# Two moves in the key scan: VectorE's product of slot 20 and GpSimd's page of slot 17

## The reference, cut to what matters

```python
z = x @ w_in                               # q | k | v | B | C | h
att  = block-sparse attention with ALiBi over q, k, v      # 8 heads x 64
conv = B * dwconv3_causal(C * h)                           # the mixer
x1 = layer_norm(alpha * x + concat(att, conv) @ w_out)
u  = dwconv3_causal(x1 @ w_ffn_up); a, g = split(u)
y  = layer_norm(alpha * x1 + (silu(a) * g) @ w_ffn_down)
```

```python
page_sum = jnp.sum(cache_k[layer, page_table], axis=2)     # all 16 pages of a sequence
gate = einsum('bthd,bnhd->bthn', q, kmean)                 # score of each block
_, sel = lax.top_k(gate, 3)
s = einsum(q, k_g) / 8 - slope * dist;  p = softmax(s);  out = einsum(p, v_g)
```

## Time and profile before

| | before |
|---|---|
| median of 3 runs | 438.33 us (438.18 to 438.52) |
| the profiled execution | 437.8 us |
| its span, first to last instruction | 436.0 us |
| mean granted TensorE clock | 0.993 |
| TensorE busy | 412.7 us (95%) |
| VectorE busy | 294.7 us (68%) |
| ScalarE busy | 181.4 us (42%) |
| GpSimd busy | 110.8 us (25%) |
| DMA | 124.60 MB, mean 286 GB/s |

### The profile page before, as it was taken

How to read it: one execution, slowest core, us unless ns; L and a number is a source line. 1 busy time by engine, 2 the same in 40 slices (tenths; PEclk the granted TensorE clock), 3 DMA queues, 4 the chain that set the end, 5 groups by cost and what they waited for, 6 DMA issues and landing times.

```text
span 436.0 us, 8237 instructions
## 1 busy us (share of the span) xinstructions
PE 412.7 (95%) x2903; PEld 339.2 (78%) x2903; DVE 294.7 (68%) x382; ACT 181.4 (42%) x694; POOL 110.8 (25%) x133
## 2 busy tenths in 40 slices
PE   4999999999999998999999989999999999999990
PEld 4588887876876774765653479999999999999990
DVE  0498999999799976954541275666776776534437
ACT  1587569644469133112110243554455555233201
POOL 1005334995255152200000717122211220000002
PEclk9999999999999999999999999999999999999997
DMA  8999999899999999999999953665556766676002
GB/s 313 397 359 407 405 407 393 316 404 409 409 359 327 338 404 405 406 405 404 402 405 398 318 196 98 194 191 162 158 169 191 213 181 186 183 211 206 3 2 99
DMA packets 109515, 124.60 MB, mean 286 GB/s; under 512 B 5903, under 2 KB 67048, under 8 KB 109466
## 3 DMA queue, kind: packets, MB, share of 16 engines
q1 hardware_dynamic: 101138, 107.30, 70.2%
q10 hardware_dynamic: 8336, 16.78, 10.2%
HBM read 121.65 MB, written 2.61 MB: 285 GB/s over the span
## 4 chain that ended last, share of the span: by engine, by line
PE 64%; DVE 18%; DMA 5%; issue 5%; SPq 4%; POOL 2%; ACT 1%; DVEq 0%; POOLq 0%; ACTq 0%
PE ps L1821 12%; PE ps L1822 11%; PE ps L1823 11%; PE ps L1714 8%; PE ps L1608 6%; DVE qk L939 6%; DVE T L949 5%; PE ps L1437 4%; PE ps L1632 4%; PE ps L1634 3%; PE ps L1384 3%; SPq L360 2%; DMA wring<-in_cache_v 2%; DMA KV<-in_cache_k 2%; POOL x1l L612 1%
## 5 line engine op out<-in xcount | busy, mean ns | idle before, releaser
L1188 DVE TENSOR_TENSOR wlo<-KV,whi 128x2048 fp32r<-128x2048 f32 (+1 forms) x24 | 61.7, 2571 | 57.5 <-ACT whi L838 29.3
L1437 PE MATMUL ps<-xT,wring 128*128 128x264 f32 x384 | 89.6, 388 | 0.1
L1437 PEld LDWEIGHTS ps<-xT,wring 128*128 128x128 f32 x384 | 71.6, 190 | 13.6 <-issue 1.7
L1821 PE MATMUL ps<-x1h,whi 128*128 128x264 f32 x256 | 73.7, 288 | 0.2
L1822 PE MATMUL ps<-x1l,whi 128*128 128x264 f32 x256 | 72.7, 284 | 0.0
L1823 PE MATMUL ps<-x1h,wlo 128*128 128x264 f32 x256 | 72.6, 284 | 0.0
L939 DVE TENSOR_TENSOR qk<-KV,qk 128x1536 f32<-128x1536 f32 (+1 forms) x32 | 67.0, 2097 | 6.6 <-DMA KV<-in_cache_k 2.7
L669 ACT ACTIVATE qk<-qk 128x64 f32<-128x64 f32 x216 | 51.9, 245 | 29.1 <-POOL qk L560 23.1
L949 DVE TENSOR_REDUCE T<-qk 128x24 f32<-128x1536 f32 (+1 forms) x32 | 58.4, 1827 | 0.0
L1821 PE MATMUL ps<-fh,whi 128*128 128x264 f32 x176 | 50.4, 286 | 0.1
L1822 PE MATMUL ps<-fl,whi 128*128 128x264 f32 x176 | 50.0, 284 | 0.0
(11 more groups left out here) (215 smaller groups left out, 574.0 us busy)
## 6 DMA issues: line engine op xcount, KB each, us to landing
KV<-in_cache_k SPq DMA_DIRECT2D x128, 256.0 KB, 6.2
KV<-in_w_ffn_up SPq DMA_DIRECT2D x32, 512.0 KB, 4.7
KV<-in_cache_v SPq DMA_DIRECT2D x60, 256.0 KB, 7.3
wring<-in_cache_v SPq DMA_DIRECT2D x56, 256.0 KB, 6.4
KV<-in_w_ffn_down SPq DMA_DIRECT2D x8, 1408.0 KB, 6.3
wring<-in_w_in ACTq DMA_DIRECT2D x5, 2048.0 KB, 14.0
zbuf<-in_cache_v SPq DMA_DIRECT2D x12, 256.0 KB, 5.3
zbuf<-in_w_ffn_up SPq DMA_DIRECT2D x3, 1024.0 KB, 10.2
```

The lines of the kernel that those rows point to most:

```text
L1188: nc.vector.tensor_tensor(wlo[s][:, 0:n], w2[s][:, 0:n], whi[s][:, 0:n], ALU.subtract).then_inc(s_lo, 1)
L1437: ins = nc.tensor.matmul(ps[:, z_bank(n), 0:R], tile[k], xT[:, k, :], start=k == 0, stop=k == KT - 1)
L1821: nc.tensor.matmul(out, wh[k], xh[k], start=k == 0, stop=False)
```

## The change

VectorE's program no longer makes the product of slot 20 as a part of `scan(19)`, after the weights of sequences 0 and 1. It makes it right after the sums of slot 18, ahead of the wait for the denominators; the sums of slot 19 stay where they were. GpSimd's program no longer multiplies its page of slot 17 after the mixer's last small products. It does so between the mixer's third tile (t = 2) and its fourth (t = 3). Nothing is added or removed.

```diff
@@ GpSimd
             for t in range(4):
+                if t == 3:
+                    multiply_page(17)
                 pool.wait_ge(s_ze, 12 + t + 1)
                 nc.gpsimd.tensor_tensor(zT[:, 20 + t, :], zT[:, 16 + t, :], zT[:, 20 + t, :], ALU.mult).then_inc(s_ch, 1)
...
                 chain(nc.gpsimd.tensor_tensor(cus, cus, cts, ALU.add))
-            multiply_page(17)
             multiply_page(18)
@@ VectorE
             probability_sums(0)
             reduce(18)
+            multiply(20)
             denominators(0)
             sample_weights(0)
             sample_weights(1)
-            scan(19)
+            reduce(19)
             own_weights(0)
             scan(20)
```

## The result

| | before | after |
|---|---|---|
| median of 18 runs each | 437.75 us (437.12 to 438.52) | 439.12 us (438.17 to 442.75) |
| ratio, 95% interval | | 1.0043 (1.0032 to 1.0055) |
| the profiled execution | 437.8 us | 438.66 us |
| its span | 436.0 us | 436.9 us |
| mean granted TensorE clock | 0.993 | 0.994 |

The change makes the kernel slower, by 1.4 us between the medians and 1.9 us by the ratio, which is of the means (0.0043 x 437.75; interval 1.4 to 2.4). The forecast was +0.81 us, and a median of 439.1.

The account below looks back on a forecast made before the run. The prediction took the wait chain through VectorE's penalties to TensorE as the bound, DMA queues second. Delays of +0.45 and +0.36 gave +0.81 us, from a median of 438.33 to 439.1; range 437.8 to 440.1.

Parts of the forecast that it names:

- Both collisions: VectorE and GpSimd meet at slot 17 and the penalties (+0.45 us), and at slot 22's product and L591 (+0.36).
- the sum of 0.81: TensorE's delays at the penalties, +0.45, and at the first value product, +0.36, add to +0.81 us.
- How a waiting engine gets in: Between VectorE and GpSimd, the first runs to its end; the other begins about 0.14 us before that recorded end.
- Edit 1, VectorE first: VectorE's slot 17 product runs first; the mixer's late steps hold the gate penalties: +0.45 us at TensorE; forecast's chance 0.40.
- nothing there is waited for: From 100 to 119 us TensorE has only 0.04 us of idle time, so work freed there brings no gain.
- Edit 1, GpSimd first: Rival: GpSimd's L566 goes first at 93.95, slot 17's product waits, penalties 0.9 to 1.2 us late; 439.7 us, chance 0.26.
- the tie: GpSimd's instruction behind slot 17's page (93.95) and VectorE's slot 17 product (93.94) fall due within 0.02 us; VectorE favoured.
- Edit 2: the mechanism: Slot 22's product, earlier at about 124.88, holds GpSimd's L591, for which TensorE's first value product waits: +0.36 us.
- The hole in the queues: DMA rate falls to 302 GB/s from 135 to 150 us; values 4 go out later, widening it by TensorE's delay.
- Both bounds move together: Delays to TensorE between 99.67 and 136 us also delay the refilling of the DMA queues.
- The rival that the queues gain: Key loads fill the DMA hole of 135 to 150 us: -1.1 us, 437.2, chance 0.11.

Follow-up runs that it names:

- Without its collision edit 2: Only edit 2 on the kernel before, with VectorE waiting for GpSimd's products with B ahead of the product of slot 22; 437.85 us, ratio 1.0007.
- edit 2: VectorE's product of slot 20 moved right behind slot 18's sums; alone against the kernel before: 438.6 us, ratio 1.0017.
- with the penalties out of the way as well: Both edits, gate penalties ahead of slot 16's sums, and VectorE waiting ahead of slot 22's product, against the kernel before; 437.99 us, ratio 1.0009.
- edit 1: GpSimd's page of slot 17 moved ahead of the mixer's fourth tile; alone against the kernel before: 438.3 us, ratio 1.0006.
- the page alone: The kernel before with only GpSimd's page of slot 17 moved, VectorE as before; 438.3 us, ratio 1.0006.
- the deliberate delay: The kernel before with one VectorE sum of the first gate's penalties made five times instead of once; 443.3 us, ratio 1.0134.
- the run with GpSimd first at slot 17: Both edits, with VectorE's product of slot 17 waiting for the first product of the mixer's last tile, against the kernel before; 440.0 us, ratio 1.0055.
- the run with VectorE first: Both edits, with GpSimd waiting for VectorE's product of slot 17 before the mixer's last tile, against the kernel before; 439.3 us, ratio 1.0037.

## Why the prediction was right, and where its sum was not

**Direction and place: right, shown.** Both collisions are where they were put, and the waits of TensorE with them. Without its collision edit 2 costs nothing that can be measured; with the penalties out of the way as well, both edits together cost nothing that can be told from noise (+0.4 us).

**The number: near in part by luck.** 439.1 was forecast and 439.12 measured, but the forecast started from 438.33, where the kernel before has 437.75 in these runs. The loss is 1.4 to 1.9, about twice the sum of 0.81. The 0.78 at the first value product is not the sum come true either: edit 1 brought 0.43, of which 0.21 came back, and edit 2 brought 0.56 and not 0.36.

**How a waiting engine gets in: right.** L568 ends at 97.20, so it began in effect at 97.20 - 0.74 = 96.46, 0.14 ahead of the recorded end of VectorE's product (96.60). L592 began at 128.27 - 0.25 = 128.02, 0.15 ahead of 128.17. The 0.115 us behind the end that the Trainium skill gives (SBUF — State Buffer, "A bandwidth-pool intuition that's wrong (but worth ruling out)"), there for GpSimd's descriptor writing held up by a VectorE copy, is not what these rows show.

**Edit 1, VectorE first: sized right (+0.45 forecast, +0.43 measured at the penalties).** But "nothing there is waited for" between 100 and 119 was wrong in a small way: TensorE's copy of the maxima, some 6.5 us behind the penalties, had waited for VectorE before, and 0.21 of the delay comes back there. In the runs of the page alone that kept their clock, whichever engine won in them, no loss can be told (437.8 us).

**Edit 1, GpSimd first: the tie was called, its odds and its price were not.** I gave VectorE the tie because its start was recorded 0.01 earlier; that decides nothing (GpSimd won in the second profile of the same program, with the same 0.01). The forecast priced the loss at the penalties at 0.9 to 1.2, which is right (0.95 and 1.16), and stopped there. The step that failed is that the delay is all there is: TensorE's idle time ahead of the penalties grows from 0.86 to between 1.81 and 2.02, and the clock may fall after it. Of the 30 timed runs of the changed kernel, 20 have a clock of 0.990 or more and a median of 438.7 (+1.0, close to the forecast), and 10 have 0.983 to 0.989 and a median of 440.8 (+3.1). The sizes fit: the kept runs lie between the shifts of the first value product in the two profiles (0.78 and 1.30), and 1.30 with the clock's 1.7 is 3.0. Such runs occur, apart from the deliberate delay, only in kernels where GpSimd can win the tie ahead of the penalties. That runs lose their clock at the penalties is seen in one profiled execution of the page alone and one of the deliberate delay; for the changed kernel itself, whose two profiles both kept it, it is inferred.

**Edit 2: the mechanism right, the size too small (+0.36 forecast, +0.54 alone and +0.56 in the changed kernel).** That between penalties and first value product the shift grows by just 0.35 is the 0.56 less the 0.21 that comes back ahead of it. With edit 2 alone L591 ends when it was said to (127.61, or 127.14 with the start-up taken off, against 127.15); but TensorE starts 0.20 behind that end and not 0.07, and the start before was taken as 126.86 and not 126.80. The page of slot 20 took 2.85 (about 2.9 forecast), L592 1.76 (1.8), and the inverse still had 0.44 to spare, as worked out.

**A third place was passed over.** Behind the first value product I let the delay pass on unchanged. At the end of the scan VectorE's product of slot 30 and GpSimd's page of slot 31 meet. VectorE's and GpSimd's rows after:

```profile
175.50 2.65 DVE L940 TENSOR_TENSOR qk<-KV,qk 128x1536 f32<-128x1536 f32 x1
```

```profile
175.27 1.27 POOL L560 TENSOR_TENSOR qk<-KV,qk 128x512 f32<-128x512 f32 x1 [1.24 <-issue]
```

and before, VectorE and then GpSimd, where the order is the other way and the late one is GpSimd's page, which VectorE needs only for its last sums:

```profile
173.82 1.75 DVE L939 TENSOR_TENSOR qk<-KV,qk 128x1536 f32<-128x1536 f32 x1
```

```profile
174.19 2.51 POOL L560 TENSOR_TENSOR qk<-KV,qk 128x512 f32<-128x512 f32 x1 [1.84 <-issue]
```

After, TensorE waits 0.59 ahead of the second gate's sums; by the program it needs VectorE's last sums there. With edit 2 alone it waits 0.68, in the second execution of the changed kernel 0.23. But this is not the change's alone. In the second execution of the unchanged kernel GpSimd is first as well, VectorE's product is held, and TensorE waits 0.22:

```profile
174.80 2.28 DVE L939 TENSOR_TENSOR qk<-KV,qk 128x1536 f32<-128x1536 f32 x1
```

In the profile of the run with GpSimd first at slot 17 it doesn't wait at all. So the place scatters from one execution to the next, and what the change adds there is not shown. That 0.78 and 0.59 make the 1.37 between the medians is chance as far as these runs tell. Nor does everything pass on: TensorE's waits for the last values, which the sum did not look at, take something back (0.45 + 0.80 + 0.17 before and 0.70 in its second execution, 0.16 + 0.18 after).

**The hole in the queues: not shown.** It was to widen by as much as TensorE is late. Values 4 are later by 0.79 without the start-up. The stretch from 135 to 150 moves more than in the first profile before, 326 GB/s against 302, but 342 in the second, whose start-up matches: the scatter between two executions of one kernel is larger than the effect. "Both bounds move together" is therefore open. The rival that the queues gain is refuted as a net gain, since the kernel got slower. Its price was also added up unevenly: it takes 1.9 for slot 24's keys, where 118.4 against 120.1 gives 1.7.

**Open.** Why the idle time of 1.98 in one profile left the clock at 1.00 and 2.02 in another did not; why the run with VectorE first costs +1.6, of which its profile shows 1.11 at the first value product; and why the page alone, where the clock fell, costs 1.8 in the median of such runs when its profile has the first value product 2.63 later.

## What to carry to other kernels

Before you move an operation into a gap of one of two engines that hold each other up, list what the other engine runs there and what each small operation on the critical path then waits for; and follow the later times to the next place where the two engines work side by side, since a delay changes who is first there. A tie within some hundredths of a us has to be priced with both outcomes (of four profiles with this tie open, each engine won two), and the worse one includes what TensorE's idle time does to its clock. A wait taken away is worth only what the next one behind it leaves.

## What the runs showed of the hardware

- TensorE was granted 0.56 to 0.59 for about 4 us after it had stood idle for 2.02 us and again for 3.89 us; after 0.86, 1.29, 1.50, 1.81 and 1.98 us it kept 1.00 in the profiled executions.
- Two starts recorded 0.01 us apart go either way from run to run, and the one recorded first can be the one that waits (94.94 with 2.37 beside 94.95 with 0.74).
- An operation of 32x64 elements is held by GpSimd like a large one: 0.21 us undisturbed, 0.36 after, 0.68 in the run of the page alone.
- The start-up scatters by about 1 us between executions of one kernel (slot 16's product at 89.85 and 90.83 before), about as large as the effect that was to be read; counting from a common event took it out of the early times. It does not reach the end whole: of 0.98 between two executions of the kernel before, 0.26 is left at the last value product (236.70 and 236.96).
